# The sum over experts moved into the second block's program, and large buffers placed at multiples of 512 bytes

## What is computed

```python
logits = xf @ w_router + b_router
top_val, top_idx = lax.top_k(logits, 4)
gates = softmax(top_val)
hid = xb @ w_mlp1[e] + b_mlp1[e]                 # per expert e, on the rows routed to it
act = glu * sigmoid(1.702 * glu) * (lin + 1)     # glu, lin: clamped even and odd columns
y   = (act @ w_mlp2[e] + b_mlp2[e]) * gate
ffn = segment_sum(y, token)                      # four rows for each token
x   = x + gt2 * rms_norm(ffn, g_post_ffn)        # end of block one
h   = rms_norm_2(x, attn_norm_w)                 # start of block two, layer 0
proj = h @ w_in                                  # its first dense products
```

## Time and profile before

| what | us |
|---|---|
| median of 3 runs | 3333.4 (3331.82 to 3333.67) |
| the profiled execution, whole time | 3338.27 |
| its span, first to last instruction | 3336.5 |
| TensorE busy in the span | 2934.3 (88%) |
| VectorE, ScalarE, GpSimd busy | 2202.6, 1619.3, 85.8 |
| mean granted clock of TensorE | 0.91 |

### The profile page before, as it was taken

How to read it: one execution, slowest core, us unless ns; L and a number is a source line. 1 busy time by engine, 2 the same in 40 slices (tenths; PEclk the granted TensorE clock), 3 DMA queues, 4 the chain that set the end, 5 groups by cost and what they waited for, 6 DMA issues and landing times. The chain is left out here.

```text
span 3336.5 us, 41343 instructions
## 1 busy us (share of the span) xinstructions
PE 2934.3 (88%) x13577; PEld 2323.4 (70%) x13577; DVE 2202.6 (66%) x3091; ACT 1619.3 (49%) x2099; POOL 85.8 (3%) x98
## 2 busy tenths in 40 slices
PE   7766797379999999999999178889999998899998
PEld 5544565358888888888887066568888775578887
DVE  6546753469999999999998446555444455554444
ACT  5322232168888888888886042433322224432332
POOL 0000000100000000000000200000000000000000
PEclk9876658589999999999999589999999999999999
DMA  9300000279999999999996331123333321132332
GB/s 355 123 19 0 4 1 1 108 275 362 390 389 379 390 388 379 391 384 385 390 381 274 124 125 57 32 77 94 101 95 101 105 70 41 51 108 82 95 101 88
DMA packets 263765, 610.35 MB, mean 183 GB/s; under 512 B 21356, under 2 KB 113276, under 8 KB 263640
## 3 DMA queue, kind: packets, MB, share of 16 engines
q1 hardware_dynamic: 246176, 549.59, 45.0%
q0 software_dynamic: 10816, 37.11, 3.1%
q10 hardware_dynamic: 6648, 22.00, 1.6%
HBM read 583.38 MB, written 25.24 MB: 182 GB/s over the span
## 5 line engine op out<-in xcount | busy, mean ns | idle before, releaser
L1180 DVE TENSOR_TENSOR weights_low<-pieces,weights_high 128x1024 fp32r<-128x1024 f32 x768 | 891.3, 1219 | 73.6 <-ACT weights_high L1173 64.0
L1173 ACT ACTIVATE weights_high<-pieces 128x1024 fp32r<-128x1024 f32 x768 | 804.8, 1061 | 204.0 <-PE banks L373 203.1
L371 PE MATMUL banks<-weights_high,xT_high 128*128 128x512 f32 x1024 | 404.3, 395 | 1.3 <-DVE weights_low L1180 1.3
L372 PE MATMUL banks<-weights_low,xT_high 128*128 128x512 f32 x1024 | 400.4, 391 | 0.0
L373 PE MATMUL banks<-weights_high,xT_low 128*128 128x512 f32 x1024 | 400.1, 391 | 0.0
L1885 ACT ACTIVATE weights_high<-pieces 128x1024 fp32r<-128x1024 f32 x192 | 201.1, 1054 | 356.3 <-DMA pieces<-in_w_up 256.7
L1889 DVE TENSOR_TENSOR weights_low<-pieces,weights_high 128x1024 fp32r<-128x1024 f32 x192 | 233.7, 1223 | 127.7 <-ACT weights_high L1885 126.6
L371 PE MATMUL banks<-hT_high,weights_high 128*128 128x512 f32 x704 | 283.6, 403 | 2.8 <-DVE hT_low L2818 2.8
L372 PE MATMUL banks<-hT_low,weights_high 128*128 128x512 f32 x704 | 275.8, 392 | 0.0
L373 PE MATMUL banks<-hT_high,weights_low 128*128 128x512 f32 x704 | 275.3, 391 | 0.0
L371 PEld LDWEIGHTS banks<-weights_high,xT_high 128*128 128x128 f32 x1024 | 193.2, 189 | 52.7 <-issue 13.7
(11 more groups left out here) (408 smaller groups left out, 4693.4 us busy)
## 6 DMA issues: line engine op xcount, KB each, us to landing
pieces<-in_w_mlp SPq DMA_DIRECT2D x768, 512.0 KB, 7.7
pieces<-in_w_up SPq DMA_DIRECT2D x64, 512.0 KB, 4.1
pieces<-in_w_down SPq DMA_DIRECT2D x64, 512.0 KB, 3.3
pieces<-in_w_in SPq DMA_DIRECT2D x56, 512.0 KB, 5.2
pieces<-in_w_ada SPq DMA_DIRECT2D x48, 512.0 KB, 8.7
expert_out<-y ACTq DMA_DIRECT2D x32, 512.0 KB, 7.6
pieces<-in_w_out SPq DMA_DIRECT2D x16, 512.0 KB, 4.3
pieces<-in_w_o SPq DMA_DIRECT2D x8, 512.0 KB, 5.2
```

What stands on the lines that cost most here:

```text
L371: nc.tensor.matmul(out, a[0], b[0], start=start, stop=False)
L372: nc.tensor.matmul(out, a[0], b[1], start=False, stop=False)
L1173: self.core.nc.scalar.activation(self.hi[:, c % E_PARTS, :], self.raw[:, c % E_RAW, :], ACT.Copy).then_inc(self.high.sem, 1)
L1180: self.core.nc.vector.tensor_tensor(self.lo[:, c % E_PARTS, :], self.raw[:, c % E_RAW, :], self.hi[:, c % E_PARTS, :], ALU.subtract).then_ ...
```

## The change

- `moe.slots` gets ROWS = 512 rows per expert, so the scatter's indices serve for the gather too, and the second set of indices and the zeroing of gates go. The 384 rows beyond the first block of each expert are zeroed by 32 DMAs of 1.5 MB from a zero tile, issued by POOL in the MLA attention (`aside`), and POOL waits for them ahead of the scatter.
- `more_blocks_stage` stores its rows in `moe.slots` instead of adding them into `ffn`. Its memset and iota load go.
- `combine_stage` and `residual_stage` for the experts go. The second block's program gathers through 6 places; TensorE puts the bias and one row of four (times a diagonal matrix of gates, made by ACT) into PSUM, DVE adds the other three from there; norm, residual and the second block's first norm follow tile by tile, interleaved by hand in the lists of ACT and DVE.
- The gain for the norm goes through DRAM (`moe.gain`).
- The second block's ring lies over the expert ring, and SP loads its first six pieces at the end of the expert stage. Its semaphores have names of their own, and POOL clears the first block's in the expert stage; `clear_stage` goes.
- `pad_first`, `pad_experts` and `pad_second` of 384, 160 and 352 bytes bring the large buffers behind them to multiples of 512 bytes.

The diff, cut to its core:

```diff
+            if aside is not None:
+                @block.gpsimd
+                def _(pool):
+                    aside(pool)
...
+        self.slot, self.gate, self.spread, self.flag = kept
         nc = core.nc
         self.h2 = nc.dram_tensor("h2_rows", [S, D], F32).ap()
-        self.slots = nc.dram_tensor("expert_out", [E * CAP, D], F32).ap()
+        self.slots = nc.dram_tensor("expert_out", [E * ROWS, D], F32).ap()
+        self.gain = nc.dram_tensor("ffn_gain", [D], F32).ap()
+        self.zeroed = core.event("slots_zeroed")
         self.table = nc.dram_tensor("token_table", [E * ROWS, 1], F32).ap()
+        scope, core.scope = core.scope, None
         self.full = [core.event(f"weight_full{i}") for i in range(E_RAW)]
         self.high, self.low, self.used = core.event("weight_high"), core.event("weight_low"), core.event("weight_used")
+        core.scope = scope
+    def zero_later_blocks(self, pool):
+        zeros = self.core.mask[:, 0:S - P]
+        rows = (BLOCKS - 1) * CAP * D // (P * (S - P))
+        for e in range(E):
+            later = self.slots[e * ROWS + CAP:(e + 1) * ROWS, :].rearrange("r d -> (r d)").rearrange("(p b n) -> p b n", p=P, n=S - P)
+            pool.dma_start(later, zeros.unsqueeze(1).broadcast_to([P, rows, S - P])).then_inc(self.zeroed.sem, 16)
...
+            sp.dma_start(moe.gain, gate[0:1, :]).then_inc(gain_out.sem, 16)
             for k in range(E_RAW):
                 moe.load(sp, moe.first_piece(0, k), moe.first_src(W, 0, k))
+            sp.wait_ge(*gain_out(16))
...
-            step(nc.vector.tensor_scalar(placef[:], rankf[:], float(CAP), None, ALU.is_lt))
-            step(nc.vector.tensor_tensor(moe.gate[:], moe.gate[:], placef[:], ALU.mult))
-            step(nc.vector.tensor_tensor(rankf[:], rankf[:], placef[:], ALU.mult))
-            step(nc.vector.scalar_tensor_tensor(out=slotf[:], in0=slotf[:], scalar=float(CAP), in1=rankf[:], op0=ALU.mult, op1=ALU.add))
-            step(nc.vector.tensor_copy(moe.slot[:], slotf[:]))
...
+            pool.wait_ge(*moe.zeroed(16 * E))
...
+        sb("pad_experts", [P, 40])
...
+                for p in range(PLACES):
+                    sp.wait_ge(*moe.low(PER_EXPERT * E - E_RAW + p + 1))
+                    stream.load(sp, p)
...
+                for s in over:
+                    pool.sem_clear(s.sem)
...
-                    act.dma_start(moe.slots[bass.ds(e * CAP, CAP), :], y[:]).then_inc(stored.sem, 16)
+                    act.dma_start(moe.slots[bass.ds(e * ROWS, CAP), :], y[:]).then_inc(stored.sem, 16)
...
-                nc.vector.memset(more[:], 0.0)
-        load_stage(core, [(iota[:], W["iota"])], "more_loads")
...
+                            act.dma_start(moe.slots[bass.ds(e * ROWS + b * CAP, CAP), :], xg[:]).then_inc(stored.sem, 16)
...
-def experts_part(core, W, x, moe, gate):
-    experts_stage(core, W, moe)
-    with ExitStack() as inner:
-        ffn = core.sb("ffn", [P, T, D], ctx=inner)
-        more_blocks_stage(core, W, moe, ffn)
-        combine_stage(core, W, moe, ffn)
-        residual_stage(core, x, ffn, gate)
...
+ROW_PLACES, ROWS_PE = 6, 1
+ROWS_DVE = TOP_E - ROWS_PE
+SUM_BANK = (4, 6, 2, 4)
...
-        self.raw, = zone.lay(("pieces2", [P, PLACES, PIECE], F32))
+        self.raw, self.hi = zone.lay(("pieces2", [P, PLACES, PIECE], F32), ("weights2_high", [P, PLACES, PIECE], F32R))
         self.lo, = zone.lay(("weights2_low", [P, PLACES, PIECE], F32R))
-        zone.close(ctx)
-        self.hi = core.sb("weights2_high", [P, PLACES, PIECE], F32R, ctx=ctx)
...
+                for p in range(PLACES, L2 * LAYER_PIECES):
...
+                for i in range(TOP_E * T):
+                    if i == ROW_PLACES:
+                        for dst, src in loads:
+                            pool.dma_start(dst, src).then_inc(constants.sem, 16)
+                    if i >= ROW_PLACES:
+                        t, j = (i - ROW_PLACES) // TOP_E, (i - ROW_PLACES) % TOP_E
+                        pool.wait_ge(*(rows_multiplied(t + 1) if j < ROWS_PE else rows_added(ROWS_DVE * t + j - ROWS_PE + 1)))
+                    pool.indirect_dma_start(slot_rows[:, i % ROW_PLACES, :], None, moe.slots, bass.IndirectOffsetOnAxis(moe.slot[:, i // TOP_E, i % TOP_E:i % TOP_E + 1], 0)).then_inc(fetched[i % ROW_PLACES].sem, 16)
...
+                        pool.wait_ge(*(added(layer - 1, 56 + 2 * t + 2) if layer else x_new(t + 1)))
...
+                def bias_rows(t):
+                    if t == 0:
+                        pe.wait_ge(*gates_taken(1))
+                        pe.wait_ge(*ffn_loads(32))
+                    if t == 3:
+                        pe.wait_ge(*rows_added(1))
+                    for n in range(2):
+                        nc.tensor.matmul(psum[:, SUM_BANK[t] + n, :], gT[:, t, :], b2[0:E, n * BANK:(n + 1) * BANK], start=True, stop=False, skip_group_check=True)
+                def multiply_rows(t):
+                    for j in range(ROWS_PE):
+                        i = TOP_E * t + j
+                        pe.wait_ge(*diag_ready(ROWS_PE * t + j + 1))
+                        pe.wait_ge(*fetched[i % ROW_PLACES](16 * (i // ROW_PLACES + 1)))
+                        for n in range(2):
+                            last = nc.tensor.matmul(psum[:, SUM_BANK[t] + n, :], diag[:, ROWS_PE * t + j, :], slot_rows[:, i % ROW_PLACES, n * BANK:(n + 1) * BANK], start=False, stop=j == ROWS_PE - 1, skip_group_check=True)
+                    last.then_inc(rows_multiplied.sem, 1)
...
+                    else:
+                        pe.wait_ge(*(rows_added(2 * ROWS_DVE + 1) if t else gates_taken(1)))
...
+                        turn_gates()
+                        for t in range(3):
+                            bias_rows(t)
+                        for t in range(3):
+                            multiply_rows(t)
+                        bias_rows(3)
                         turn_h(0, 0)
-                        turn_h(0, 1)
+                        multiply_rows(3)
                     for s in range(SLOTS):
                         after = {k: [] for k in range(KD)}
-                        if s == 0:
-                            after[7] += [lambda: turn_h(layer, 2 if layer == 0 else 3)]
-                        if s == 1 and layer == 0:
-                            after[7] += [lambda: turn_h(0, 3)]
+                        if s == 0 and layer:
+                            after[7] += [lambda: turn_h(layer, 3)]
+                        if s < 2 and layer == 0:
+                            after[7] += [lambda t=t: turn_h(0, t) for t in ((1,), (2, 3))[s]]
...
+                act.dma_start(b2[0:E, :], W["b_mlp2"][0]).then_inc(ffn_loads.sem, 16)
+                act.dma_start(ffn_gain[:], moe.gain.partition_broadcast(P)).then_inc(ffn_loads.sem, 16)
+                act.wait_ge(*gates_turned(1))
+                nc.scalar.activation(gT.rearrange("e t p -> e (t p)"), psum[0:E, 0, :], ACT.Copy).then_inc(gates_taken.sem, 1)
+                for t in range(T):
+                    for j in range(ROWS_PE):
+                        nc.scalar.activation(diag[:, ROWS_PE * t + j, :], ident[:], ACT.Copy, scale=moe.gate[:, t, j:j + 1]).then_inc(diag_ready.sem, 1)
...
+                square_ffn(0)
+                square_ffn(1)
+                root_ffn(0)
+                square(0, 0)
+                square_ffn(2)
+                root_x(0, 0)
+                root_ffn(1)
+                copy_h(0, 0)
+                square(0, 1)
+                square_ffn(3)
+                root_x(0, 1)
+                root_ffn(2)
+                copy_h(0, 1)
+                square(0, 2)
+                root_x(0, 2)
+                root_ffn(3)
+                copy_h(0, 2)
+                square(0, 3)
+                root_x(0, 3)
+                copy_h(0, 3)
...
+                def add_rows(t):
+                    for j in range(ROWS_PE, TOP_E):
+                        i, n = TOP_E * t + j, ROWS_DVE * t + j - ROWS_PE
+                        dve.wait_ge(*fetched[i % ROW_PLACES](16 * (i // ROW_PLACES + 1)))
+                        dve.wait_ge(*(rows_added(n) if j > ROWS_PE else rows_multiplied(t + 1)))
+                        to = psum[:, SUM_BANK[t]:SUM_BANK[t] + 2, :].rearrange("p b n -> p (b n)") if j == ROWS_PE else ffn[t]
+                        nc.vector.scalar_tensor_tensor(out=ffn[t], in0=slot_rows[:, i % ROW_PLACES, :], scalar=moe.gate[:, t, j:j + 1], in1=to, op0=ALU.mult, op1=ALU.add).then_inc(rows_added.sem, 1)
+                def mean_ffn(t):
+                    dve.wait_ge(*ffn_squares(t + 1))
+                    nc.vector.tensor_scalar(ffn_mean[:, t:t + 1], ffn_ms[:, t:t + 1], 1.0 / D, EPS, ALU.mult, ALU.add).then_inc(ffn_spread.sem, 1)
+                def add_ffn(t):
+                    dve.wait_ge(*ffn_rooted(t + 1))
+                    step(nc.vector.reciprocal(ffn_root[:, t:t + 1], ffn_root[:, t:t + 1]))
+                    if t == 0:
+                        dve.wait_ge(*ffn_loads(32))
```

(38 more changed lines are left out.)

222 lines of the change are left out of this document (80 added, 142 removed).

## The result

The changed kernel takes 3342.3 us (median of 15 runs, 3334.3 to 3347.4) against 3332.7 us before (15 runs, 3329.7 to 3338.3): ratio 1.0027, 95% interval 1.0019 to 1.0035. It is 9.6 us slower where the forecast said 39 faster. The profiled execution has a span of 3344.5 us at a mean clock of 0.909, 8.0 us more than before.

The account below looks back on a forecast made before the run. The hand-over from experts to second block was taken as serial DVE, DMA and barrier work, 104 us. 3338.3 - 40.8 + 2 = 3299.5 profiled; the median of runs lies 4.9 lower: 3294 us, range 3288 to 3302.

Parts of the forecast that it names:

- the new start: Hand-over after the experts: the second program starts at B = 1840.5, after store landing, one barrier, flag and branch.
- the chain: Hand-over steps after B: first dense product at 47.4, third group at 76.2, which is 40.8 us earlier than before.
- the row on TensorE: Hand-over sums: TensorE's diagonal products take one row of four, 3.5 us a tile; DVE does 12 additions instead of 16.
- The zeros: MLA attention: 32 added stores, 50.3 MB, drain hidden and POOL's issue below 3.1 us each; 2 us charged for key positions.
- the key load: Load of key positions issued at 398, 3.0 us alone; sharing DMA engines with the stores adds 2 us (ends 0 and 4).
- the landing: Drain of the zero stores from the MLA attention: 32768 packets at 65 ns, 133 us, from about 298 to 431.
- break-even: Rival in the MLA attention: POOL holds the stage and 33 to 39 us come back, 3327 to 3333; chance 0.08.
- POOL can't run ahead of a drain: One of two causes in the break-even rival: the 133 us drain holds POOL in MLA attention; chance 0.08 for both.
- The same with DVE in the way: Rival in the MLA attention: 5.3 us an issue beside DVE, 70 beyond the stage, 31 slower than before, 3364; chance 0.08.
- The loads weren't late: Judges the hand-over rival that bias and gain loads land at 10 instead of 6.5, gathers at 8: 3306; chance 0.10.
- TensorE's clock: Hand-over sums: 0.50 assumed; rival at full clock has six bias products in 5.3 instead of 10.5 us: 3286; chance 0.11.
- the multiples of 512: Buffer starts for expert and second-block products: taken as 0; rival that alignment counts, 61 us more gained, 3233, chance 0.03.

Follow-up runs that it names:

- Tile by tile: Changed kernel with 16 stores each in MLA and DSA attention; TensorE does bias then row per tile, bias products wait for the bias load alone: 3285.1 us, ratio 0.9855.
- 24 and 8: Changed kernel with 24 of the 32 zero stores in the MLA attention and 8 in the DSA attention: 3306.1 us, ratio 0.9918.
- wide pieces: Changed kernel with all 32 stores in the MLA attention, each as 128 pieces of 12288 bytes instead of 1024 of 1536: 3314.3 us, ratio 0.9952.
- SP's stores: Changed kernel with all 32 zero stores in the DSA attention, issued by SP's queue instead of POOL's: 3320.9 us, ratio 0.997.

## Why the prediction was wrong

- **Right, the new start.** The forecast had 5.7 us from the last expert product to the second program; POOL's first gather stands 5.9 behind it, at 1890.45. That is B below.
- **Right, the chain.** Bias products from B + 6.9 (6.5), 10.58 us for six (10.5); VectorE's first addition at B + 21.3 (20.6); first dense product at B + 46.7 (47.4); third group at B + 77.0 (76.2). The diagonal products took 1.64 each against 1.75. That no wait on a weight piece stands there was right; that the early load was what hid the 12.24 us was not, for without it the third group moves by 0.8.
- **Right, but for the wrong reason: the row on TensorE.** The text counted 12 instead of 16 additions as a saving. The chain with the row was priced correctly; the chain without it was never worked out, and it is 3.8 us shorter. Tile by tile the row costs 0.5: it was the order of TensorE's list that the text didn't question.
- **Wrong, and the whole miss: "The zeros".** The step asked one question, what an issue costs POOL, and its answer was good (0.88 us against "below 3.1"). It let the transfers drain until 431 and looked for who waits for them: the scatter at 638.9 and the key load. It left out the stage itself. The stage ends when POOL's stores have landed, also when POOL has long issued the last (24 and 8; wide pieces). The price was therefore not the issues but the landing: the stage lasts 152.1 us instead of 99.6, 52.5 more. The text had both numbers, 133 us of draining and 99.6 us of stage, and let only POOL's issues, not the landing, hold the stage; the 33 us between them stand in a rival alone.
- **Mis-sized within it: the landing.** 133 us came from 32768 packets of 1536 bytes at 65 ns, which is 378 GB/s, off a line through one point of each kind of queue. There were 11776 packets of 4274 bytes, and they moved at 359 GB/s, 140 us; the dips at POOL's stops and the two ends make it 151.7. With 133 the rival gave 33 us back, measured were 52.5: that is the difference between its "break-even" and a slower kernel. The 2 us for the key positions were nothing: their load took 3.0 us as before, behind the stores.
- **The rivals.** "POOL can't run ahead of a drain" was the nearest, at 0.08 for two causes together. Half of it holds: POOL stops after 15 stores. But wide pieces, and 24 and 8, show that most of the time doesn't hang on that. The argument against it, one cheap indirect gather with 128 pieces, speaks of issues and says nothing of 50 MB. The Trainium skill (DMA: Bandwidth & Descriptors, Anatomy of one DMA) says that many descriptors can be emitted before their cost shows; the trace agrees for 15 stores of 1024 pieces, and no further. "The same with DVE in the way" doesn't hold: between 300 and 310 us DVE was busy 9.24 of 10, and the issues took 0.88 each, not 5.3. The loads weren't late: the gain landed after 6.7 us (6.5 in the forecast), the gathers after a median of 6.1 (5.4). That rival's price was added up wrongly: 3.5 + 2 x 2.6 and as much again is 17, so 3312 and not 3306; it decides nothing. TensorE's clock rose only in part, to 0.60 over the rows of the first two tiles (1908 to 1915).
- **Right by luck: the multiples of 512.** Between before and after the term is 0. But the pads are not idle: without them the new tiles put the operands of the second block 160 bytes apart, and the kernel is 30 us slower. The row behind the 0 compared two places in which both operands happened to start at the same offset, 480 and 480, 128 and 128, so it could not show what a difference costs.
- **Not shown**: by what mechanism POOL's end of a stage waits for landings, what sets its stop after 15 stores, and why the offsets matter; only that they do.

## What to carry to other kernels

For transfers moved "beside" a stage, compare their landing time, bytes over the measured rate, with the stage's length, and ask whose queue issues them: in these runs POOL's held the end of the stage until they had landed, SP's held SP at the issue; spread over two stages with room the same stores cost nothing. Before giving an engine part of another's work, work out the chain without it too, at the clock the helper will have, and see in which order the helper's list lets the first result out. And when tiles are added or dropped, keep both operands of the products at the same offset within 512 bytes.

## What the runs showed of the hardware

- POOL's queue took 15 stores of 1024 pieces in 13.3 us and no 16th for another 57 us, until DMA had nearly run dry; of stores with 128 pieces it took 32 in 16.9 us.
- A stage in which POOL had issued stores ended only when DMA had gone quiet: at 449.0 (issued by 439.6), 411.4 (by 376.1) and 423.5 (by 315.7). With SP's stores the next stage started with 3.4 MB still to move.
- SP's queue held SP for 4.0 us on average at each store of 1024 pieces of 1536 bytes (32 in 128.6 us).
- The same 50.3 MB of stores, away from the dips, ran at 359 GB/s in 11776 packets (POOL, pieces of 1536 bytes), at 368 GB/s (SP) and at 419 GB/s in 4608 packets (POOL, pieces of 12288 bytes).
- At full clock these products of 512 columns come every 0.2267 us with both operands at the same offset within 512 bytes (0, 32, 128, 480 by the allocations), and every 0.232 to 0.234 us with a difference of 64 or 160 bytes.
